# Attention statistics and bias moved by GpSimd, a third PSUM bank for the head tiles, probabilities turned one slot later

## The reference

```python
h = rms_norm(x, norm_mix_pre)
q, k, v, glu_in, gates = split(h @ w_in)          # 12 heads of 128, 3 groups of 4
a = dilated_attention(q, k, v, rel_bias)          # groups (window, dilation) = (128,1), (512,4), (2048,16)
y_a = a @ w_attn_out
c = c_val * sigmoid(c_gate)                       # from glu_in
c = silu(layer_norm(causal_depthwise_conv(c)))    # 31 taps
y_c = c @ conv_pw_w
x = x + rms_norm((sigmoid(g_a) * y_a + sigmoid(g_c) * y_c) @ w_out)
x = x + rms_norm(feed_forward(rms_norm(x)))
```

## Time and profile before

| | us |
|---|---|
| median of 3 runs | 1669.93 (1669.73 to 1672.88) |
| the profiled execution | 1670.05 |
| its span (first to last instruction) | 1668.2 |
| around the span | 1.85 |
| heads, from 804 to 1161 us of the span | 357 |

### The profile page before, as it was taken

One profiled execution on the slowest core, in us unless ns is written; L12 is line 12 of the kernel. 1 busy time (PEld: TensorE's weight loads), 2 busy tenths in 40 slices (PEclk: granted clock), 3 DMA queues, 4 the chain that ended last, 5 costly groups with the idle time before them and its releaser, 6 DMA issues.

```text
span 1668.2 us, 24134 instructions
## 1 busy us (share of the span) xinstructions
PE 1594.0 (96%) x9246; PEld 1410.1 (85%) x9246; DVE 1111.4 (67%) x1543; ACT 551.5 (33%) x743; POOL 20.6 (1%) x38
## 2 busy tenths in 40 slices
PE   7999999899999999999998989989998999999995
PEld 7999999899999988778886877877786888887884
DVE  5334455689888832387998888765556898887323
ACT  5123333342222222243333323547333322222321
POOL 1100000000000000000000000000000000000001
PEclk9999999899999999999999999999998999999998
DMA  4442212123222333313322323222322323323331
GB/s 166 124 123 94 88 56 89 58 93 98 88 88 88 97 96 110 101 64 100 98 88 69 95 63 83 77 65 88 101 89 63 102 90 99 101 89 100 102 111 65
DMA packets 50047, 152.50 MB, mean 91 GB/s; under 512 B 10714, under 2 KB 12262, under 8 KB 49984
## 3 DMA queue, kind: packets, MB, share of 16 engines
q1 hardware_dynamic: 41760, 147.26, 28.3%
q0 software_dynamic: 1120, 3.23, 0.8%
q10 hardware_dynamic: 7104, 1.12, 0.7%
HBM read 149.44 MB, written 4.51 MB: 92 GB/s over the span
## 4 chain that ended last, share of the span: by engine, by line
PE 78%; DVE 15%; ACT 4%; issue 1%; DMA 1%; ACTq 0%; DVEq 0%; SPq 0%
PE ps L443 75%; DVE work L1417 6%; DVE wlo L1088 2%; ACT whi L753 1%; DVE res L1160 1%; DVE tmp L1156 1%; ACT probs L954 1%; DMA raw<-w_dram 1%; PE ps L630 1%; PE ps L703 1%; DVE peaks L1461 1%; PE ps L541 1%; DVE acc L1129 1%; ACT L1013 0%; PE ps L691 0%
## 5 line engine op out<-in xcount | busy, mean ns | idle before, releaser
L443 PE MATMUL ps<-xh,whi 128*128 128x258 f32 (+2 forms) x2048 | 582.1, 333 | 20.4 <-DVE wlo L1088 9.1
L443 PE MATMUL ps<-xh,wlo 128*128 128x258 f32 (+2 forms) x2048 | 574.3, 329 | 0.0
L443 PE MATMUL ps<-xl,whi 128*128 128x258 f32 (+2 forms) x2048 | 574.2, 329 | 0.0
L1088 DVE TENSOR_TENSOR wlo<-raw,whi 128x1024 fp32r<-128x1024 f32 x272 | 331.8, 1220 | 185.3 <-ACT whi L753 184.8
L753 ACT ACTIVATE whi<-raw 128x1024 fp32r<-128x1024 f32 x272 | 287.0, 1058 | 438.8 <-DMA raw<-w_dram 438.7
L443 PEld LDWEIGHTS ps<-xh,whi 128*128 128x128 f32 x2048 | 349.2, 191 | 54.5 <-issue 21.7
L443 PEld LDWEIGHTS ps<-xh,wlo 128*128 128x128 f32 x2048 | 348.2, 191 | 34.3
L443 PEld LDWEIGHTS ps<-xl,whi 128*128 128x128 f32 x2048 | 349.1, 191 | 31.9 <-issue 0.2
L1417 DVE SCALAR_TENSOR_TENSOR work<-cin,vecs,work 128x512 f32<-128x512 f32 x240 | 180.1, 750 | 6.9
L443 PE MATMUL ps<-fh,whi 128*128 128x512 f32 x352 | 137.1, 389 | 2.5 <-DVE stage L1174 1.3
L443 PE MATMUL ps<-fl,whi 128*128 128x512 f32 x352 | 137.0, 389 | 0.0
(11 more groups left out here) (198 smaller groups left out, 1494.7 us busy)
## 6 DMA issues: line engine op xcount, KB each, us to landing
raw<-w_dram SPq DMA_DIRECT2D x272, 512.0 KB, 3.5
bias_copies_dram<-bias_rows_dram POOLq DMA_DIRECT2D x12, 192.0 KB, 3.7
res<-x_dram SPq DMA_DIRECT2D x8, 264.0 KB, 6.6
out_dram<-res SPq DMA_DIRECT2D x8, 256.0 KB, 2.0
dftp<-dftp_dram POOLq DMA_DIRECT2D x1, 550.7 KB, 4.6
bias<-bias_copies_dram ACTq DMA_DIRECT2D x4, 128.0 KB, 4.9
bias<-bias_copies_dram ACTq DMA_DIRECT2D x8, 64.0 KB, 5.2
vecs<-vec_dram SPq DMA_DIRECT2D x1, 364.0 KB, 8.6
```

The costliest lines, as they stand in the source:

```text
L443: last = pe.matmul(ps[:, bank, 0:b - a], w[:, slot, cols], xx[:, k, a:b], start=start and n == 0, stop=stop and n == 2)
L1088: dve.tensor_tensor(wlo[:, slot, :], raw[:, slot, :], whi[:, slot, :].bitcast(F32), ALU.subtract).then_inc(w_split, 1)
```

## The change

- ScalarE no longer stores and loads statistics or loads bias. GpSimd has a loop over the four heads instead: wait until the bias tile is free (`max_ready`), load the head's bias (three transfers), wait for all eight exponentials, store the statistics (two), wait until they have landed, load them back (two). The wait for `stats_stored` goes with them.
- Tiles go to banks 0, 2, 3 in rotation, and tile n waits until tile n - 3 has been read.
- The values are turned in bank 1 alone, so each `turn_values` waits until ScalarE has copied back the one before it.
- `turn_probs`, `turned_probs`, `weigh_values` and `attention_hi`/`attention_lo` each come one slot later.

```diff
+TILE_BANKS = (0, 2, 3)
@@ GpSimd
+            for j in range(HEADS):
+                if j:
+                    pool.wait_ge(max_ready, 2 * j)
+                else:
+                    pool.wait_ge(operand_ready, READY["x2"])
+                load_bias(j)
+                pool.wait_ge(exp_ready, 8 * (j + 1))
+                for kind in range(2):
+                    pool.dma_start(stats_rows(kind == 0, 2 * SEQ * kind), head_stats[:, 0, 4 * kind:4 * kind + 4, :]) \
+                        .then_inc(stats_stored, 16)
+                pool.wait_ge(stats_stored, 32 * (j + 1))
+                for kind in range(2):
+                    pool.dma_start(head_stats[:, 1, 4 * kind:4 * kind + 4, :],
+                                   stats_rows(kind == 0, 2 * SEQ * (1 - kind))).then_inc(stats_landed, 16)
@@ TensorE
-                if NG * j + g >= 2:
-                    pe.wait_ge(v_back, NG * j + g - 1)
+                if NG * j + g >= 1:
+                    pe.wait_ge(v_back, NG * j + g)
                 for kb in range(QB):
-                    last = pe.transpose(ps[:, 1 + 2 * ((NG * j + g) % 2), kb * P:(kb + 1) * P],
+                    last = pe.transpose(ps[:, 1, kb * P:(kb + 1) * P],
-                    j = head_at(n, 5 + t)
+                    j = head_at(n, 6 + t)
                     if j is not None:
                         turn_probs(j, t)
-                    j = head_at(n, 6 + t)
+                    j = head_at(n, 7 + t)
                     if j is not None:
                         weigh_values(j, t)
-                one_piece_tile("heads", n, n % 4, 2 * (n % 2), n - 1, (xh2, xl2), row2, middle=lambda: mid_tile(n))
+                one_piece_tile("heads", n, n % 4, TILE_BANKS[n % 3], n - 2, (xh2, xl2), row2, middle=lambda: mid_tile(n))
@@ ScalarE
-            act.wait_ge(bias_spread, 16 * NG * HEADS)
-            load_bias(act, 0)
-                if head_at(n, 8) is not None:
-                    attention_hi(head_at(n, 8))
+                if head_at(n, 9) is not None:
+                    attention_hi(head_at(n, 9))
                     exps(j, 1)
-                    store_stats(j)
-                    if j < HEADS - 1:
-                        load_bias(act, j + 1)
-                if head_at(n, 2) is not None:
-                    load_stats(head_at(n, 2))
-                    if head_at(n, 4 + t) is not None:
-                        turned_probs(head_at(n, 4 + t), t)
+                    if head_at(n, 5 + t) is not None:
+                        turned_probs(head_at(n, 5 + t), t)
@@ VectorE
-                waits = any(head_at(n, off) is not None for off in (0, 1, 8))
+                waits = any(head_at(n, off) is not None for off in (0, 1, 9))
-                if head_at(n, 8) is not None:
-                    attention_lo(head_at(n, 8))
+                if head_at(n, 9) is not None:
+                    attention_lo(head_at(n, 9))
```

More of the change, by code:

```diff
@@ L358, in stats_rows @@
             return bass.AP(stats_dram.tensor, offset, [[2 * R, P], [2, R], [1, 2]])
[L360 to L367, removed]
         block = ctx.enter_context(nc.Block())
@@ L426, in _, with load_bias @@
             pool.wait_ge(bias_spread, 16 * NG * HEADS)
+            def load_bias(j):
+                for g in range(NG):
+                    c0, c1 = ((0, 256), (256, 384), (384, 512))[g]
+                    pool.dma_start(
+                        bias[:, c0:c1],
+                        bass.AP(bias_copies.tensor, (g * HEADS + j) * P * BIAS_W + P - 1,
+                                [[BIAS_W - 1, P], [1, c1 - c0]])).then_inc(bias_landed, 16)
+            for j in range(HEADS):
[12 more added lines that the diff above has]
+                                   stats_rows(kind == 0, 2 * SEQ * (1 - kind))).then_inc(stats_landed, 16)
             pool.wait_ge(rstd_ready, 6)
@@ L956, in exps @@
                        .then_inc(exp_ready, 1)
[L958 to L969, removed]
             def exp_shares(j):
@@ L994, in _ @@
                     act.wait_ge(v_turned, NG * j + g + 1)
-                    act.activation(qkv[j % 2][:, g, :], ps[:, 1 + 2 * ((NG * j + g) % 2), :], ACT.Copy) \
+                    act.activation(qkv[j % 2][:, g, :], ps[:, 1, :], ACT.Copy) \
                        .then_inc(v_back, 1)
@@ L1005, in _ @@
                     act.activation(qkv[n // 9 % 2][:, n % 9, :].rearrange("p (r l) -> p r l", r=R),
-                                   tile_psum(2 * (n % 2), False).rearrange("p (l r) -> p r l", r=R), ACT.Identity) \
+                                   tile_psum(TILE_BANKS[n % 3], False).rearrange("p (l r) -> p r l", r=R), ACT.Identity) \
                        .then_inc(tile_read, 1)
                 elif n < 9 * HEADS:
-                    act.activation(qkv[n // 9 % 2][:, n % 9, :], tile_psum(2 * (n % 2), False), ACT.Identity) \
+                    act.activation(qkv[n // 9 % 2][:, n % 9, :], tile_psum(TILE_BANKS[n % 3], False), ACT.Identity) \
                        .then_inc(tile_read, 1)
@@ L1012, in _ @@
                     t = n - 9 * HEADS
-                    act.activation(gates2[:, t, :], tile_psum(2 * (n % 2), False), ACT.Sigmoid,
+                    act.activation(gates2[:, t, :], tile_psum(TILE_BANKS[n % 3], False), ACT.Sigmoid,
                                    bias=vec("b_gate_2", t)) \
```

## The result

| | before | after |
|---|---|---|
| median, us | 1669.83 (5 runs, 1669.73 to 1672.88) | 1655.93 (5 runs, 1654.99 to 1661.33) |
| span of the profiled execution, us | 1668.2 | 1655.0 |
| TensorE's granted clock, mean, as a share of full speed | 0.981 | 0.982 |

The ratio is 0.992, with a 95% interval from 0.9902 to 0.9937: 13.9 us less between the medians, 13.2 between the profiled spans. The forecast was 1655.3. A second set of runs of the same kernel gave 1657.04.

What follows compares the result with a forecast made beforehand. TensorE, 96% busy, bounds the kernel, with VectorE close in the heads phase. Of 26.2 us of stalls and clock loss, new losses of 11.45 leave 14.75 us gain: 1670.05 - 14.75 = 1655.3 us, forecast 1648 to 1663 (0.50), range 1645 to 1676.

Steps and rivals of the forecast that it cites:

- waits for the probabilities: TensorE's four waits in the heads phase, one per head, 15.7 us in all, claimed to go with the later slot.
- slot 13's turn, and the clock behind: First head: TensorE waits 3.2 us for ScalarE's copy of slot 12's turn, instead of 3.69; 1.6 us clock loss stays.
- slot 14's turn: First head's third value turn: waits 0.65 us for a copy behind `exp_shares`, which needs the statistics.
- slots 22 and 23: Second head's value turns: waits of 2.0 and 2.5 us for ScalarE's copies, with no clock loss.
- last head: Copy of the first turned part stands behind slot 41's `conv_out`, which waits for VectorE's last tap: 1.5 us, from 0 to 3.
- C: Time from a head's last exponential to its statistics' landing through GpSimd's transfers, taken at 9 us, 4.5 each way.
- VectorE's gap at piece 14: VectorE's 4.00 us gap shrinks to 1.5, as ScalarE's read, and so the next weight piece's conversion, comes 2.5 us earlier.
- What could be won: TensorE's stalls and clock losses in the heads phase: 15.7 + 3.7 + 1.6 + 5.2 = 26.2 us.
- The 15 ns a piece of the upper bound: Assumed cost per transfer piece: a store of 512 pieces lands after 9.4 us, store and load take 19 us.
- The rule against it: The skill says VectorE's two-port operations lock out GpSimd's descriptor writing, so the statistics' travel would grow; no size given.
- Rival 2: VectorE becomes the bound in the first two heads, giving 1657.2 us; chance counted within the forecast's 0.50.
- Rival 3: Slow statistics hold ScalarE's `exp_shares` and copies behind it; gain gone at C = 12, 1682 us at 15; slower: chance 0.18.

Runs made afterwards that it cites:

- the best kernel: Kernel after with old banks, slot 41's convolution output late, first head's attention_lo ahead of the taps, second exponentials a slot later in three heads: 1650.18 us, ratio 0.9886.
- the longer way: Kernel after plus one DRAM-to-DRAM transfer of the statistics that GpSimd issues and waits for between store and load: 1669.79 us, ratio 0.999.

## Why the prediction was right

Step by step, predicted against measured:

| step | predicted | measured |
|---|---|---|
| waits for the probabilities | 15.7 to 0 | 0 |
| slot 13's turn, and the clock behind | 3.2 and 1.6 | 2.92 and 1.6 |
| slot 14's turn | 0.65 | none |
| slots 22 and 23 | 2.0 and 2.5 | 1.73 and 2.06 |
| slots 31 and 32 | 0 | none |
| last head | 1.5 | 2.70, and about 1.3 of clock |
| C | 9 | 7.7, 8.9, 9.7, 9.7 |
| VectorE's gap at piece 14 | 4.0 to 1.5 | 1.34 |

- *What could be won.* The later slot takes all four stalls, and banks or GpSimd alone do not, as the kernels with one part show. This step held. That all three parts are needed does not: two of them reach the same time.
- *The new wait at the old place.* Slot 13 was right to 0.3 us, and so was its reason: the copy stands behind the exponentials, a read and a conversion. With old banks the wait falls to 1.1.
- *The travel time.* It was bounded from 4 to 19 and taken at 9. The first head's 7.7 left TensorE no wait in slot 14. The 15 ns a piece of the upper bound were far off: GpSimd issued the two stores, of 512 and 128 pieces, in 1.31 us, and in the second and the last head the store of 512 pieces landed 4.1 and 2.8 us after its issue, sooner than the one of 128 behind it (5.0 and 4.1).
- *The rule against it.* VectorE was busy 61.66 and 62.91 us of 65 and 67, and GpSimd's stores still landed within 3.5 to 4.7 us of their issue's end. The Trainium skill (SBUF — State Buffer, "SBUF: two separate sides") ties the holding up of descriptors to VectorE's operations in a two-port mode; two inputs in SBUF take the lock only against a GpSimd operation that reads SBUF. Most of VectorE's time here goes to the taps, which have two inputs, and nothing here shows them holding a transfer up.
- *The last head* was sized too low: 1.5 for 2.70 and a slow clock behind it. ScalarE waits 5.98 us there for VectorE's last tap, with the copy behind:

```profile
1082.70 0.72 ACT L957 ACTIVATE cin<-work,vecs 128x512 f32<-128x512 f32 x1 [5.98 <-DVE work L1413]
...
1084.84 0.48 ACT L981 ACTIVATE pt<-ps 128x384 f32<-128x384 f32 x1
```

- *The balance.* Waits 9.4, clock 1.6 + 1.3, and 1.6 behind the phase's end, which the prediction didn't have: 13.9 of loss, so 26.2 - 13.9 = 12.3 by the rows against 13.2 of span. The 0.9 is not assigned. That the sum met the median within 0.6 us is partly luck: the new losses were 2.5 us higher than the 11.45 predicted. The sum stood on a slot 14 wait of 0.65 that did not come, and had 1.2 too little for the last head's wait and nothing for the clock behind that wait and behind the phase's end.
- *Rival 2* (VectorE bounds the phase) is not borne out: the best kernel runs TensorE at 63.50 of 65 us there, with VectorE at 60.38, though 2.3 us of waits for VectorE's probabilities are left in its first two heads. *Rival 3* has the right mechanism, as the longer way shows, and its point of 12 is near the 12.6 at which the gain was gone; GpSimd's transfers just didn't get there.

## What to carry to other kernels

A wait on an in-order engine is also a wait of everything listed behind it: before a buffer is taken from one use for another, look up where the copy that frees it stands in its engine's list, and behind which waits. The worth of a part depends on what else is in: here the bank exchange alone gained nothing, cost 5.7 us on top of the later slot, and so raised what GpSimd's part was worth from 8.3 to 11 or 12, while the later slot and GpSimd without the banks did as well as all three. The later slot and GpSimd each pay alone (7.7 and 6.7 us), and together a little more than their sum (16.0). When a stall goes, look at the place where it was for the next in line, and price it by the time when that one becomes free, not by zero. And when a small move gains more than the wait that it removes, look at the granted clock before calling it scatter.

## What the runs showed of the hardware

- The clock behind a short stall isn't a matter of the stall's length alone. The granted clock fell behind waits of 2.97 and 2.92 us and not behind one of 3.08 (before, third head). A wait of 2.12 to 2.15 us stands at the phase's end in all thirteen profiles: the clock stayed full behind it in seven (the kernel before among them) and fell in six, both of the kernel after among them. There it cost about 1.6 us: the next matmuls start 0.43 us apart instead of 0.23. What decides is open.
- The fall can come late. With the probabilities later alone, TensorE went on at full speed for 1.5 us behind the 2.94 us wait of slot 22, and then ran eight matmuls 0.43 us apart.
- On ScalarE's queue the small stores landed later with bias loads right behind them. In the kernel before the stores of the first three heads landed 4.7 to 6.4 us after their issue, those of the last head, with nothing behind, 2.8 and 3.1. It is not a rule without exceptions: with the probabilities later alone the last head's took 3.7 and 6.4. On GpSimd's queue, with nothing behind the stores, they took 2.8 to 5.0; the loads, which have bias loads behind them, landed in 1.8 to 2.3 us in the first two heads and 3.9 and 4.0 in the third, in two of three heads no slower than those of the last head (2.4 and 3.5), which have none. So leaving ScalarE's queue is not by itself the faster way: from the last exponential to the issue of the loads it took 6.1, 5.3, 6.9 and 3.5 us there, and 5.1, 6.3, 5.1 and 5.4 on GpSimd's. The first head's rows of the kernel after:

```profile
880.90 1.31 POOL L437 DMA_DIRECT2D stats_dram<-head_stats  x2 [154.38 <-ACT probs L968]
885.68 1.29 POOL L441 DMA_DIRECT2D head_stats<-stats_dram  x2 [3.47 <-DMA stats_dram<-head_stats]
```

GpSimd takes longer to issue two stores (1.31 us against 0.94). The heads differ in time and in the other traffic as well, and no kernel changed what stands behind the stores alone, so the cause of the longer landings is not shown.
